# A backbone step with product-key experts: the prompt tile's routing taken between the convolution's taps instead of between the q and k units

## The reference, cut to what matters

```python
def trunk_layer(x, mod, lp, l, ctx):
    h = modulate(x, lp['norm1_g'], sh1, sc1)
    y, new_ctx = mixer(h, lp, l, ctx)          # pool, neighbourhood attention, convolution, differential attention, merge
    x = x + g1 * y
    h = modulate(x, lp['norm2_g'], sh2, sc2)
    x = x + g2 * peer_ffn(h, ...)              # product-key routing, top-k gather of experts
```

```python
s1, i1 = lax.top_k(s[:, :, 0], PEER_TOPK)
s2, i2 = lax.top_k(s[:, :, 1], PEER_TOPK)
cand = (s1[..., :, None] + s2[..., None, :]).reshape(-1, PEER_HEADS, PEER_TOPK * PEER_TOPK)
sc, ci = lax.top_k(cand, PEER_TOPK)
e = take_along_axis(i1, ci // PEER_TOPK) * PEER_NKEYS + take_along_axis(i2, ci % PEER_TOPK)
```

## Time and profile before

| | |
|---|---|
| median of three runs | 5236.48 us |
| the profiled execution | 5236.58 us, span 5234.8 us |
| TensorE busy | 4471.4 us, 85% of the span |
| VectorE busy | 3365.5 us, 64% |
| ScalarE busy | 1876.5 us, 36% |
| GpSimd busy | 1776.3 us, 34% |
| DMA | 1677.26 MB, 320 GB/s mean |
| granted TensorE clock, mean | 0.959 of full speed |
| chain that ended last | DMA 39%, TensorE 34%, VectorE 14%, ScalarE 7%, issue 5% |

### The profile page before, as it was taken

One profiled execution on the slowest core, in us unless ns is written; L12 is line 12 of the kernel. 1 busy time (PEld: TensorE's weight loads), 2 busy tenths in 40 slices (PEclk: granted clock), 3 DMA queues, 4 the chain that ended last, 5 costly groups with the idle time before them and its releaser, 6 DMA issues.

```text
span 5234.8 us, 46808 instructions
## 1 busy us (share of the span) xinstructions
PE 4471.4 (85%) x14388; PEld 2309.5 (44%) x14388; DVE 3365.5 (64%) x7265; ACT 1876.5 (36%) x5016; POOL 1776.3 (34%) x1600
## 2 busy tenths in 40 slices
PE   7789988998799888888888898999879987777777
PEld 3584455334546443335544444643454532222222
DVE  2426765777777677675444487777777767676544
ACT  0210143343233433565533113544323343333333
POOL 2105301333243453443333270223224444444332
PEclk9799988998899999999999998999989999999999
DMA  8462216999799999999999220299979999999998
GB/s 321 168 207 90 82 49 234 339 359 351 275 420 420 415 419 420 413 399 419 407 417 419 95 97 33 74 355 351 360 277 420 420 413 421 421 421 419 417 422 358
DMA packets 277115, 1677.26 MB, mean 320 GB/s; under 512 B 31809, under 2 KB 31857, under 8 KB 112385
## 3 DMA queue, kind: packets, MB, share of 16 engines
q0 software_dynamic: 190896, 1365.43, 64.4%
q1 hardware_dynamic: 82944, 302.03, 15.9%
q10 hardware_dynamic: 3024, 6.82, 0.3%
HBM read 1667.33 MB, written 6.82 MB: 320 GB/s over the span
## 4 chain that ended last, share of the span: by engine, by line
DMA 39%; PE 34%; DVE 14%; ACT 7%; issue 5%; POOL 0%; SPq 0%; DVEq 0%; ACTq 0%; POOLq 0%; PEldq 0%
DMA arena<-experts,bsb 26%; PE ps L2185 12%; DMA arena<-experts,peidx 11%; PE ps L1773 7%; DVE arena L1676 3%; PE ps L1947 3%; PE ps L1881 2%; DVE arena L1378 2%; PE ps L2037 2%; DMA wring<-w 2%; PE ps L2059 2%; ACT L1042 1%; ACT T L1046 1%; PE ps L1749 1%; PE ps L2076 1%
## 5 line engine op out<-in xcount | busy, mean ns | idle before, releaser
L2185 PE MATMUL ps<-arena,T 128*128 128x512 f32 x4096 | 1963.7, 612 | 443.8 <-ACT T L1046 442.2
L1676 DVE CUSTOM_DVE_ANT_0 arena<-arena,h_sb 128x1024 f32<-128x1024 f32 x1024 | 1253.0, 1227 | 862.7 <-DMA arena<-experts,bsb 857.0
L661 POOL DMA_INDIRECT arena<-experts,bsb x1024 | 1097.6, 1072 | 1724.8 <-PE ps L2185 1581.2
L2185 PEld LDWEIGHTS ps<-arena,T 128*128 128x128 f32 x4096 | 722.8, 191 | 1568.6 <-ACT T L1046 953.0
L1042 ACT ACTIVATE bsb<-T 128x1 f32<-128x1 f32 x1024 | 205.9, 201 | 1324.2 <-DVE T L1676 1322.6
L1773 PE MATMUL ps<-h_sb,wring 128*128 128x256 f32 (+2 forms) x2304 | 529.5, 388 | 33.4 <-DVE h_sb L1416 13.7
L2096 PE MATMUL ps<-h_sb,wring 128*128 128x512 f32 x1024 | 473.9, 617 | 60.7 <-DVE arena L1601 58.1
L644 POOL DMA_INDIRECT arena<-experts,peidx x256 | 287.6, 1123 | 689.3 <-DVE arena L1378 635.3
L1773 PEld LDWEIGHTS ps<-h_sb,wring 128*128 128x128 f32 x2304 | 388.7, 199 | 186.2 <-issue 150.7
L1046 ACT ACTIVATE T<-ident,bsb 128x128 f32<-128x128 f32 x1024 | 411.0, 401 | 33.5
L1368 DVE CUSTOM_DVE_ANT_0 arena<-arena,h_sb 128x1024 f32<-128x1024 f32 x256 | 313.2, 1224 | 145.2 <-DMA arena<-experts,peidx 143.8
(11 more groups left out here) (319 smaller groups left out, 4453.0 us busy)
## 6 DMA issues: line engine op xcount, KB each, us to landing
wring<-w SPq DMA_DIRECT2D x576, 512.0 KB
arena<-experts,bsb POOLq DMA_INDIRECT x1024
bsb<-bias POOLq DMA_DIRECT2D x16, 512.0 KB, 3.8
arena<-subk POOLq DMA_DIRECT2D x4, 1024.0 KB, 10.5
arena<-v_scratch POOLq DMA_DIRECT2D x64, 64.0 KB, 2.0
arena<-experts,peidx POOLq DMA_INDIRECT x256
x_sb<-xT POOLq DMA_DIRECT2D x1, 2048.0 KB, 14.1
v_scratch<-arena ACTq DMA_DIRECT2D x8, 256.0 KB, 2.0
```

What stands on the lines that cost most here:

```text
L661: gp.indirect_dma_start(rows[:, n % NS, :], None, experts, bass.IndirectOffsetOnAxis(ap=eidx[:, t % 2, i:i + 1], axis=0)).then_inc(row_in[ ...
L1676: v.tensor_tensor_reduce(e, e, htok(t), 1.0, 0.0, ALU.mult, ALU.add, dots[:, t % 2, i:i + 1]).then_inc(dot, 1)
L2185: mm = pe.matmul(ps[:, 6 + half, :], diag[:, n % ND, :], rows[:, n % NS, D + half * 512:D + (half + 1) * 512], start=(i == 0), stop=(i == ...
```

## The change

The routing generator is made ahead of the taps. One of its steps follows each of the 120 `scalar_tensor_tensor` taps, and two instead of nine follow each `qk_norm`. Since other instructions now tick VectorE's own semaphore between taps, each tap waits for the recorded count of its channel's last tap instead of a count three back.

```diff
--- before.py
+++ after.py
@@ -1453,16 +1453,21 @@
                     wait_freed(v, u(f"ca{c}"))
                     v.sem_inc(u_ready, 1)
 
+                routing_steps = prompt_route(l)
+                tap = [0] * 4
                 for k in range(CONV_W):
                     for c in range(4):
                         if k:
 
-                            v.wait_ge(dve_own, own.n - 3)
+                            v.wait_ge(dve_own, tap[c])
                             col = S_CW + c * CONV_W + k
                             op = v.scalar_tensor_tensor(acc[:, c, :], U[:, c, 1 + k:1 + k + LAT], S(col), acc[:, c, :], ALU.mult, ALU.add)
                         else:
                             op = v.tensor_scalar(acc[:, c, :], U[:, c, 1:1 + LAT], S(S_CW + c * CONV_W), S(S_CB + c), ALU.mult, ALU.add)
                         own.tick(op)
+                        tap[c] = own.n
+                        if k:
+                            next(routing_steps, None)
                 own.wait()
                 v.sem_inc(conv_done, 1)
 
@@ -1521,13 +1526,12 @@
                     own.link(v.reciprocal(rs, rs))
                     v.tensor_tensor(acc, acc, rs.unsqueeze(1).broadcast_to([P, 4, LAT]), ALU.mult).then_inc(cnorm, 1)
 
-                routing_steps = prompt_route(l)
                 for n in range(NQ + 1):
                     if n < NQ:
                         qk_mean(n)
                     if n >= 1:
                         qk_norm(n - 1)
-                        for _ in range(9):
+                        for _ in range(2):
                             next(routing_steps, None)
                     if n == LNM_AT:
                         conv_centre()
```

## The result

The changed kernel takes 5289.85 us (median of four runs, 5287.75 to 5300.57) against 5234.94: a ratio of 1.0102, 95% interval 1.0088 to 1.0116. It is 55 us slower. A repeat beside the last experiments gave 1.0093 (1.0065 to 1.0120). The forecast was 5289, slower.

The account below looks back on a forecast made before the run. VectorE and TensorE were full during the taps, TensorE's 7.31 us units the bound behind them. Per layer 57.7 - 26.0 - 5.4 = 26.3 us, 52.6 for two, on 5236.48: 5289 us, range 5256 to 5318.

Parts of the forecast that it names:

- The price of the steps: Tap stage: the 120 routing steps moved between taps add their own VectorE time, 43.8 us a layer.
- GpSimd's holds: Tap stage: steps open gaps, GpSimd's pooling gets in and makes taps wait, 13.9 us a layer.
- What follows the taps: TensorE resumes 5.6 us after the taps, then 7.31 us units; unit 15 ends 109.0 us after them, against 135.0.
- The tail: Unit 15 to first score: nine routing steps ahead of the last norm are gone, 5.4 us sooner a layer.
- X: Growth of the tap stage in a layer, steps plus GpSimd's delays: 43.8 + 13.9 = 57.7 us.
- the units: TensorE's qk units behind the taps, run without VectorE's routing in the way: 26.0 us given back a layer.
- The signs that the prediction named: Changed profile: taps about 140 us, longest near 1.7, first copy about 1, pooling over by about 500, unbroken TensorE units.
- No contention: Rival, tap stage: GpSimd slips through without holding taps; X 43.8, +12.4 us a layer, 5261 us; chance 0.15.
- Whole-instruction holds: Rival, tap stage: GpSimd holds VectorE for each whole instruction; X 69.2, +37.8 us a layer, 5312 us; chance 0.2.
- Steps hidden in the taps' ends: Rival, tap stage: steps cost 0.16 us less each; X 24.6, -6.8 us a layer, 5223 us; chance 0.04.
- The order makes no difference: Rival: moved steps free as much behind the taps as they cost before; X about 31, 5237 us; chance 0.03.

Follow-up runs that it names:

- e1: Changed kernel, but GpSimd starts a layer's latent pooling only after the last tap; 5278 us, ratio 1.0068 to the kernel before.
- e2: Changed kernel with the same 120 routing steps in one block ahead of the 120 taps; 5272 us, ratio 1.0053 to the kernel before.
- e3: Changed kernel with 60 steps between the taps and five behind each norm, instead of 120 and two; 5262 us, ratio 1.0039 to the kernel before.
- e4: Kernel before, no steps between taps; 67 steps behind norms by a price table, 73 behind the first 23 attention jobs; median 5285 us, ratio 1.0083.
- e9: Kernel before with 27 steps behind the last tap, 88 behind norms, the rest in a block (8 us) and behind six attention jobs; 5215 us, ratio 0.9952.

## Why the prediction was right

**The price of the steps.** 43.8 us by the start-to-start prices; 42.9 in e1, where nothing else is in the way. That is 0.36 us a step, as counted, and 2% under the sum.

**GpSimd's holds.** 13.9 predicted, 12.5 measured (135.1 less 122.6). The forecast of each kind was near: a window sum made a tap 1.30 to 1.37 instead of 0.73 (0.57 to 0.64, where 0.67 was said; 1.58 in one of ten), the subtraction 1.49 to 1.58 (0.8, where 0.85 was said), the scaling 0.82 to 0.89 (0.1 to 0.16, where 0.2 was said). Summed over the tap records of layer 0, what is over 0.73 us is 3.2 us beside the four subtractions (3.4 predicted), 6.2 beside the ten window sums (6.7), 2.1 beside the eight bias additions (2.2) and 1.0 beside scalings and copies (1.6). That e1 removes just this, by moving GpSimd alone, is what makes the mechanism shown and not argued. The rule of the Trainium skill (SBUF — State Buffer, Who interferes with whom), that the later instruction is blocked until the other is finished, would have given 25.4 us by the prediction's count, twice what was measured. The trace agrees that the two engines keep each other out, and disagrees with the length: no kind of instruction held a tap for its whole duration, the scaling least of all.

**What follows the taps.** TensorE resumed 5.7 us behind the first mean, predicted 5.6. The first unit with its transposes took 10.2 us, much of it at the lower clock level (granted clock 0.72), instead of the 8.8 taken from a row behind a short gap. So unit 15 ended 110.6 us behind the first mean, not 109.0. From there on it ran 7.30 us units without a gap, as said: TensorE was the bound that the reading had made it.

**The tail.** Norm 15 follows norm 14 directly (685.10 behind 683.52). Unit 15 to first score is 12.9 us instead of 17.5; predicted 12.1. The pooling products ran for 5.44 us at a granted clock of 0.66 where the kernel before had 4.52 at 0.79. In layer 1 the kernel before had 19.2 us there, so 6.3 came back and not 4.7; the prediction had priced one layer and doubled it.

**The sum.** The tap stage grew by 55.5 us in layer 0, TensorE's units gave back 24.5 and the tail 4.7: 26.3 us, against 57.7 - 26.0 - 5.4 = 26.3 predicted. Three terms were off by one to two microseconds (X by -2.2, the units by +1.5, the tail by +0.7) and cancelled. The total of 55 is 2 us over the forecast's 52.6, though the two stretches hold only 51.2 of it and the rest lies in stages that the change does not touch. The closeness of the 5289 is luck at that scale; the range was 62 us wide. The signs that the prediction named came true: the taps ran for 136 us (about 140 was said), the first copy took 0.61 us, pooling was over at 478 us, the longest tap took 1.58 us, and TensorE had no idle time between q and k units behind the first.

**The rivals.** No contention: excluded by e1. Whole-instruction holds: excluded by the tap durations. Steps hidden in the taps' ends: excluded by e1, 0.36 us a step where the break-even is 0.26 (no row shows the 0.16 us less that this rival supposed), and by e2, where the block costs no more or less than the interleaved steps once holds are taken off. The order makes no difference: excluded by the stretches of the changed kernel, e1, e2 and e3, 8 to 26 us longer.

What is open: why TensorE's clock fell in the second layer's attention of e4 and, less, in the first layer's of e1, e2 and e9 and not in others. The runs show that it happens with and without steps there. It was worst in one layer of e4, which had the most steps, and hardly there in its other layer, which had the same steps. All six timed runs of e4 took 5260 us or more, so it is not one bad execution. The cause stays open.

## What to carry to other kernels

Work moved off a busy stretch must be weighed by who waits behind its new place: between the taps it delayed the engine that was the bound afterwards, behind the norms it was mostly covered. Count the idle time behind each step of the bound engine and hand out the filler by that, instead of an equal number to each, which was worth 25 us here. Alternating one-input and two-input VectorE work lets GpSimd in between, so a GpSimd queue that was starved for free begins to cost, here 12.5 us of the 55.5 that the tap stage grew by.

## What the runs showed of the hardware

- Back-to-back two-input VectorE instructions keep a GpSimd copy of 0.61 us waiting for 75.15 us; a single MAX8 of 0.28 us between two of them is enough to let it in.
- A GpSimd addition of 1.09 us alone, once in, makes the next two-input VectorE instruction about 0.6 us longer; a GpSimd scaling of 1.49 us only 0.1 to 0.16.
- Attention with the same matmuls took 164 us at a granted clock of 0.98 in its second part and 225 at 0.70 and 0.52, with TensorE busy for 90% of the time and more. These 61 us are more than the whole change cost. Small additions of work to VectorE stood ahead of it, and the same additions stood in layer 0, where the clock stayed at 0.93.
